# Transposing the inverse factors on VectorE in 32x32 blocks instead of on TensorE

## The chip, the cores and the metric

The kernel runs on one core of a Trainium2 chip. The metric is device time in microseconds, the median of three runs. TensorE, VectorE, ScalarE and GpSimd run side by side; SyncE issues loads. In the trace PE is TensorE, DVE VectorE, ACT ScalarE and POOL GpSimd.

## The reference

The program is three blocks one after the other on 256 tokens of width 2048: a gated delta network, a gated feed-forward, and a hybrid layer. The change lies in the first, in the part that solves a unit lower triangular system for each of 32 heads and each chunk of tokens:

```python
idx = jnp.arange(C)
lower = idx[:, None] >= idx[None, :]
strict = idx[:, None] > idx[None, :]
...
L = jnp.where(strict, jnp.einsum('bhnid,bhnjd->bhnij', kb, k) * decay, 0.0)
rhs = jnp.concatenate([v * beta[..., None], kb * jnp.exp(gc)[..., None]], -1)
sol = lax.linalg.triangular_solve(L + jnp.eye(C, dtype=L.dtype), rhs, left_side=True,
                                  lower=True, unit_diagonal=True)
```

The kernel works on chunks of 128 tokens and inverts I + L by levels: it knows the inverse on the diagonal blocks of size 1, and a level s = 2, 4, ..., 64 makes from the inverse on blocks of size s the one on blocks of size 2s, as T - T (L T) restricted to the new corner.

## The kernel before

**Stages.** The delta network's projection is walked in groups of 24 weight chunks. A chunk is 24 matmuls of 128x128 by 128x256 (or 12 of 128x512, lines 936, 923 and 955). Weights come as fp32 and are split: ScalarE copies a chunk to its high part (`gh`, line 1599), GpSimd subtracts it for the low part (`low`, line 662, `wl = wr - wh`), and TensorE multiplies with both. Buffers of high and low parts are three deep (`RING`), so the copy for chunk c + 3 waits for TensorE to have finished chunk c, and chunk c of the next group waits for GpSimd.

**Delta iterations.** Beside the chunks of group j + 1 runs the delta step of group j, eight iterations in all (`delta` on each engine). TensorE takes one chunk, one delta step, one chunk, and so on (`beside`, line 1182), with three chunks without a step behind them. In the seven first iterations all of this sits under the next group's projection; in the last one under the output projection. In-between work stands on the other engines in a fixed order written by hand: VectorE does its part of a delta step, then at steps 5 to 7 and 13 to 15 four operations of the convolution (`conv`, line 2158), then at steps 2 to 15 one mod half, two scalar_tensor_tensor of 128x512 that sum a modulation row out of SBUF (`mods`, line 2087). ScalarE does its chunk copy and then its delta part at the times in `STEP_AT`. GpSimd does the low part and at every second time issues a load of modulation weights (line 651).

**The levels.** For 4 heads and 2 token chunks there are 8 matrices, index n. `Tc` and `Uc` hold the two diagonal 64-blocks of the inverse and of its transpose, `lTb` the transposed L, `Xc` the intermediate. Blocks b = 0, 1 lie in partitions 0 to 63 and 64 to 127. Per level s, TensorE does an X step (line 1078: 16 products of 64x64), VectorE masks it from PSUM to `Xc` (line 2241, name `x`), TensorE multiplies `Uc` with it (line 1096, name `tx`), VectorE subtracts it from `Tc` (line 2246, name `t`), and TensorE transposes the new `Tc` (line 849, name `u`) in the step that also holds the next level's X; ScalarE brings the transpose from PSUM into `Uc` (line 1713). At s = 32 the transposition is done in blocks of 64 (line 1108). Before level 2 the first factors are made: `lm` masks L into `Uc` (line 2223), TensorE flips it (`flip_blocks`, line 1059, name `t2`), VectorE subtracts it from the identity into `Tc` (line 2233) and subtracts `Uc` from the identity in place (line 2236, `uc`).

**Quarters.** A 64x64 product uses the quarter of TensorE's array given by the partitions it reads and those it writes. `crossed` puts the results of level 2 in the half they came from, so only two quarters work; from level 4 on, block b of matrix n is put in half n % 2, so all four work in turn.

## Time and profile before

| | us |
|---|---|
| median of three runs | 2718.45 (2718.34 to 2719.01) |
| the profiled execution, first to last instruction | 2717.0 |
| TensorE busy (matmuls) | 2678.4 |
| VectorE busy | 1909.8 |
| ScalarE busy | 1212.6 |
| GpSimd busy | 854.2 |
| an iteration of the delta stage, second to seventh | 96.6 |

The eight delta iterations lie between about 160 and 930 us. TensorE's granted clock is full through the whole execution. A timeline row is a merged run of instructions of one kind: its length goes from the first start to the last end, and matmuls overlap, so the spacing of starts says more than the lengths. A matmul on fp32 data counts as two instructions.

### The profile page before, as it was taken

Reading aid. Unit: us, or ns where it says so; the run is one execution under the profiler, and the core shown is the slowest. Engines: PE = TensorE matmul, PEld = TensorE weight load, DVE = VectorE, ACT = ScalarE, POOL = GpSimd, SP = SyncE. Lnnn points to the kernel's source line nnn. Section 1 sums busy time; section 2 is a strip of 40 time slices with the busy share of each in tenths; the row PEclk is TensorE's granted clock in tenths of the full one; section 3 lists DMA queues with packets and bytes.
Section 4 is the critical chain, followed back from the end, with each engine's and each line's share of the span. In section 5 each row is a group of like instructions: output and inputs, shape, how many; then the busy total and the mean of one; then the engine's idle time right before and its main releaser. Section 6 shows DMA issues by size and latency. Waiting matters only on the chain.

```text
span 2717.0 us, 45293 instructions
## 1 busy us (share of the span) xinstructions
PE 2678.4 (99%) x17387; PEld 2250.4 (83%) x17387; DVE 1909.8 (70%) x2190; ACT 1212.6 (45%) x1572; POOL 854.2 (31%) x646
## 2 busy tenths in 40 slices
PE   6999999999999999999999999999999999999998
PEld 4798998899898888888888888889777778888887
DVE  1476777787787687666666666588999997655554
ACT  2355455545546445333333333354433334444344
POOL 1076676676667412600000000004565550000000
PEclk9999999999999999999999999999999999999999
DMA  9966666676665676666666666655555556666664
GB/s 364 354 219 207 227 225 204 223 239 200 224 229 188 219 223 228 189 187 186 187 190 188 190 186 186 185 162 172 171 179 170 161 173 187 192 186 186 192 202 155
DMA packets 283976, 552.53 MB, mean 203 GB/s; under 512 B 16882, under 2 KB 54323, under 8 KB 282675
## 3 DMA queue, kind: packets, MB, share of 16 engines
q1 hardware_dynamic: 263488, 473.49, 56.5%
q0 software_dynamic: 19472, 76.06, 7.4%
q8 instruction: 116, 1.90, 0.3%
q10 hardware_dynamic: 866, 0.80, 0.1%
q14 instruction: 34, 0.27, 0.0%
HBM read 548.19 MB, written 2.10 MB: 203 GB/s over the span
## 4 chain that ended last, share of the span: by engine, by line
PE 96%; DMA 2%; DVE 1%; SPq 1%; ACT 0%; issue 0%; DVEq 0%
PE pg L1220 40%; PE pd L1220 18%; PE pg L936 13%; PE pg L923 6%; PE pg L1207 4%; PE pg L955 3%; PE pd L849 2%; DMA wr<-in_gdn_w_in 1%; PE pd L1096 1%; PE pd L1078 1%; PE pd L1415 1%; PE pd L1428 1%; DMA arena<-in_mod_w 1%; PE pg L849 1%; PE pd L1027 1%; PE pd L1010 1%
## 5 line engine op out<-in xcount | busy, mean ns | idle before, releaser
L2341 DVE TENSOR_TENSOR wl<-wr,wh 128x1024 fp32r<-128x1024 f32 x615 | 773.7, 1268 | 453.7 <-ACT wh L1818 451.2
L1818 ACT ACTIVATE wh<-wr 128x1024 fp32r<-128x1024 f32 x616 | 652.8, 1061 | 936.2 <-PE pg L1220 590.3
L662 POOL TENSOR_TENSOR wl<-wr,wh 128x1024 fp32r<-128x1024 f32 x195 | 478.9, 2458 | 366.3 <-ACT wh L1599 231.3
L1220 PE MATMUL pg<-wh,hh 128*128 128x512 f32 x1344 | 529.8, 394 | 0.3 <-DVE hl L2414 0.3
L1220 PE MATMUL pg<-wl,hh 128*128 128x512 f32 x1344 | 527.3, 392 | 0.0
L1220 PE MATMUL pg<-wh,hl 128*128 128x512 f32 x1344 | 525.7, 391 | 0.0
L1599 ACT ACTIVATE wh<-wr 128x1024 fp32r<-128x1024 f32 x216 | 227.7, 1057 | 356.4 <-PE pg L936 196.4
L1220 PEld LDWEIGHTS pg<-wh,hh 128*128 128x128 f32 x1344 | 252.6, 188 | 59.1 <-DVE wl L2341 2.4
L936 PE MATMUL pg<-hh,wh 128*128 128x256 f32 x1024 | 300.7, 294 | 0.8 <-ACT arena L1659 0.8
L1220 PEld LDWEIGHTS pg<-wh,hl 128*128 128x128 f32 x1344 | 252.5, 188 | 56.3
L1220 PEld LDWEIGHTS pg<-wl,hh 128*128 128x128 f32 x1344 | 252.3, 188 | 53.9
L936 PE MATMUL pg<-hl,wh 128*128 128x256 f32 x1024 | 290.2, 283 | 0.0
L936 PE MATMUL pg<-hh,wl 128*128 128x256 f32 x1024 | 290.0, 283 | 0.0
L2087 DVE SCALAR_TENSOR_TENSOR arena<-arena,condt 128x512 f32<-128x512 f32 x225 | 250.2, 1112 | 20.3 <-DMA arena<-in_mod_w 14.8
L819 POOL COPY arena<-arena 128x2048 f32<-128x2048 f32 x1 | 2.7, 2662 | 671.9 <-PE pd L849 671.9
L936 PEld LDWEIGHTS pg<-hh,wh 128*128 128x128 f32 x1024 | 196.6, 192 | 16.3 <-issue 7.2
L936 PEld LDWEIGHTS pg<-hl,wh 128*128 128x128 f32 x1024 | 197.0, 192 | 0.5 <-issue 0.2
L936 PEld LDWEIGHTS pg<-hh,wl 128*128 128x128 f32 x1024 | 196.7, 192 | 0.0
L1220 PE MATMUL pd<-wl,hgh 128*128 128x512 f32 x320 | 125.5, 392 | 0.0
L1220 PE MATMUL pd<-wh,hgh 128*128 128x512 f32 x320 | 125.5, 392 | 0.0
L1220 PE MATMUL pd<-wh,hgl 128*128 128x512 f32 x320 | 125.1, 391 | 0.0
L773 POOL DMA_DIRECT2D xT<-in_final_g x1 | 0.6, 572 | 340.3 <-PE pd L1220 340.3
(446 smaller groups left out, 4727.3 us busy)
## 6 DMA issues: line engine op xcount, KB each, us to landing
wr<-in_w_in SPq DMA_DIRECT2D x224, 512.0 KB, 3.8
wr<-in_ffn_w_gu SPq DMA_DIRECT2D x176, 512.0 KB, 3.8
wr<-in_gdn_w_in SPq DMA_DIRECT2D x128, 512.0 KB, 4.1
arena<-in_mod_w POOLq DMA_DIRECT2D x60, 1024.0 KB, 6.7
wr<-in_ffn_w_down SPq DMA_DIRECT2D x88, 512.0 KB, 4.6
arena<-in_mod_w SPq DMA_DIRECT2D x32, 1024.0 KB, 13.7
wr<-in_gdn_w_in SPq DMA_DIRECT2D x128, 256.0 KB, 3.1
wr<-in_gdn_w_out SPq DMA_DIRECT2D x56, 512.0 KB, 4.5
```

What stands on the lines that cost most here:

```text
L662: nc.gpsimd.tensor_tensor(wl[c % RING][:], wraw[c % 4], wh[c % RING][:].bitcast(F32), ALU.subtract)\
L849: return nc.tensor.transpose(dst, src, ident[0:n, 0:n])
L923: m = nc.tensor.matmul(halves(bank)[:, t, :], h_s[x][:, 2 * kp + k, t * P:(t + 1) * P], w[c % RING][:, k, :], skip_group_check=True, start ...
L936: m = nc.tensor.matmul(bank[:, n * T:(n + 1) * T], w[c % RING][:, k, n * P:(n + 1) * P], h_s[x][:, 2 * kp + k, :], skip_group_check=True, ...
L955: m = nc.tensor.matmul(halves(pg[g])[:, h, :], o_s[x][:, 2 * kp + k, h * P:(h + 1) * P], w[c % RING][:, k, :], skip_group_check=True, star ...
L1010: m = nc.tensor.matmul(pd[0][:, n * 512:(n + 1) * 512], ones[:], sqb[:, n * 512:(n + 1) * 512], start=True, stop=True)
L1207: m = nc.tensor.matmul(bank[:, n * T:(n + 1) * T], w[s][:, k, n * P:(n + 1) * P], act[x][:, k0 + k, :], skip_group_check=True, start=(firs ...
L1220: m = nc.tensor.matmul(halves(bank)[:, h, :], act[x][:, k0 + k, h * P:(h + 1) * P], w[s][:, k, :], skip_group_check=True, start=(first and ...
L1599: a(wh[c % RING][:], wraw[c % 4], ACT.Copy).then_inc(s_hi, 1)
L1818: a(wh[c % 4][:], wraw[c % 4], ACT.Copy).then_inc(s_hc, 1)
L2087: m = stt(out=dst, in0=mw[t % 2][:, k, :], scalar=condt[:, kk:kk + 1], in1=dst, op0=ALU.mult, op1=ALU.add)
L2341: v.tensor_tensor(wl[c % 4][:], wraw[c % 4], wh[c % 4][:].bitcast(F32), ALU.subtract).then_inc(s_lc, 1)
```

## The change

Up to blocks of 32, the transpose of `Tc` is made by VectorE with one instruction that transposes every 32x32 block where it stands: the factors have nothing outside their diagonal 32-blocks then. The transposed factors stand in `Us`, the right half of `Ub`. TensorE reads a factor from `Us` where block b and half n % 2 agree, and else from `Uc`, where ScalarE puts it by two copies that cross the partition halves (`cross`). Products of level 2 use the same placement as the later ones. The flip of the first factor and the transpositions after t2, t4, t8 and t16 go from TensorE's program; with two results fewer per level, `pd[1]` always holds X and `pd[0]` the product. The masked L goes to `Us`, the identity is subtracted there (`us1`), and VectorE transposes it to `Tc`. The name and wait lists (`PEO`, `VO`, `AO`) change with it. Level 32 and what follows stay.

```diff
-PEO = order("ssq", "rows", "gram", "ktok", "t2", "x2", "tx2", "u2", "x4", "tx4", "u4", "x8",
-            "tx8", "u8", "x16", "tx16", "u16", "x32", "tx32", "u32", "x64", "ux64", "v0", "md0", "s", "o0", "r",
-            "qs", "v1", "o1", "md1")
-VO = order("qn", "qkn", "dt", "lt", "lm", "at", "tc", "uc", *[f"{a}{s}" for s in LEVELS for a in ("x", "t")],
+PEO = order("ssq", "rows", "gram", "ktok", "vt1", *[f"{a}{s}" for s in LEVELS for a in ("x", "tx")],
+            "u32", "x64", "ux64", "v0", "md0", "s", "o0", "r", "qs", "v1", "o1", "md1")
+VO = order("qn", "qkn", "dt", "lt", "lm", "at", "us1", "tc",
+           *[f"{a}{s}" for s in LEVELS for a in (("x", "t", "us") if s < 32 else ("x", "t"))],
            "x64", "u64", "md0", "o0", "rhs1", "o1", "oz", "md1", "on", "og")
-AO = order("rnq", "rn", "exp", "kg", "vtok", "z", *[f"u{s}" for s in LEVELS], "v0", "s", "qs", "v1", "qkv", "rstd")
+AO = order("rnq", "rn", "exp", "kg", "vtok", "u1", "z", *[f"u{s}" for s in LEVELS], "v0", "s", "qs", "v1", "qkv", "rstd")
 GO = order("rowm")
...
@@ -222,6 +222,7 @@
         Tb = take(8, P)
         Xc = Xb.rearrange("p a b -> p (a b)")[:, 0:512].rearrange("p (n t) -> p n t", t=64)
         Ub = take(8, P)
+        Us = Ub[:, :, 64:P]
         Tc, Uc = (Tb.rearrange("p a b -> p (a b)")[:, 512 * i:512 * (i + 1)].rearrange("p (n t) -> p n t", t=64)
                   for i in range(2))
...
@@ -1036,7 +1037,6 @@
                     m = tr(pd[0][:, 512 + h * P:512 + (h + 1) * P], vT[:, h, 0:P])
                 m.then_inc(s_pe, 1)
                 yield
-                V("lm")
                 Ac("kg")
 
...
-                def crossed(s, b, n):
-
-                    return (b, slot(n)) if s == 2 else (n % 2, 4 * b + n // 2)
+                def crossed(b, n):
+
+                    return n % 2, 4 * b + n // 2
+
+                def u_block(b, n):
+
+                    r = slice(64 * (n % 2), 64 * (n % 2) + 64)
+                    return Us[r, n, :] if n % 2 == b else Uc[r, n // 2, :]
 
                 def each_block():
                     for m in range(4):
                         yield from ((0, 2 * m), (1, 2 * m + 1), (0, 2 * m + 1), (1, 2 * m))
 
-                def flip_blocks(bank, src, at):
-                    for n in range(8):
-                        for b in range(2):
-                            r = slice(64 * b, 64 * b + 64)
-                            m = nc.tensor.matmul(block(bank, b, slot(n)), src[r, at(n), :], ident[r, r],
-                                                 start=True, stop=True)
-                    return m
-                flip_blocks(pd[0], Uc, slot)
...
-                par = 1
...
                     else:
                         for b, n in each_block():
                             r = slice(64 * b, 64 * b + 64)
-                            m = nc.tensor.matmul(block(pd[par], *crossed(s, b, n)), lTb[r, n, r], Tc[r, n, :],
+                            m = nc.tensor.matmul(block(pd[1], *crossed(b, n)), lTb[r, n, r], Tc[r, n, :],
                                                  start=True, stop=True)
...
                 for s in LEVELS:
                     V(f"x{s}")
-                    if s > 2:
-                        Ac(f"u{s // 2}")
-                    else:
-                        V("uc")
+                    Ac(f"u{s // 2}")
+                    if s == 2:
                         Ac("vtok")
-                    par ^= 1
                     for b, n in each_block():
-                        half, i = crossed(s, b, n)
+                        half, i = crossed(b, n)
                         r = slice(64 * half, 64 * half + 64)
-                        m = nc.tensor.matmul(block(pd[par], b, slot(n)), Uc[r, i, :], Xc[r, i, :], start=True, stop=True)
+                        m = nc.tensor.matmul(block(pd[0], b, slot(n)), u_block(b, n), Xc[r, i, :], start=True, stop=True)
                     m.then_inc(s_pe, 1)
                     yield
                     V(f"t{s}")
-                    par ^= 1
-                    if s < 32:
-                        for m in range(4):
-                            t = tr(pd[par][:, m * P:(m + 1) * P], Tc[:, 2 * m:2 * m + 2, :])
-                    else:
+                    if s == 32:
                         for n in range(8):
...
                         for n in range(0, 8, 2):
-                            t = nc.tensor.matmul(pd[par][0:64, 512 + 32 * n:576 + 32 * n], Tc[64:P, n, :],
+                            t = nc.tensor.matmul(pd[1][0:64, 512 + 32 * n:576 + 32 * n], Tc[64:P, n, :],
                                                  ident[64:P, 64:P], start=True, stop=True)
-                    t.then_inc(s_pe, 1)
-                    par ^= 1
+                        t.then_inc(s_pe, 1)
...
@@ -1700,25 +1686,29 @@
                     a(kg0[:, h, :], pd[0][:, (h // 2) * P:(h // 2 + 1) * P], ACT.Copy, scale=tkc[:, 6, h:h + 1])
                 a(vtok[:, 0:VH, :].rearrange("p a b -> p (a b)"), pd[0][:, 512:1024], ACT.Copy).then_inc(s_a, 1)
                 yield
-                V("tc")
+                PEw("vt1")
                 a(vtok[:, VH:8, :].rearrange("p (a b) t -> p a (b t)", a=2),
                   pd[0][:].rearrange("p (a c) -> p a c", a=2)[:, :, 256:512], ACT.Copy).then_inc(s_a, 1)
+
+                def cross(s):
+
+                    V(f"us{s}")
+                    a(Uc[0:64, 0:4, :], heads(Us)[64:P, :, 0, :], ACT.Copy)
+                    a(Uc[64:P, 0:4, :], heads(Us)[0:64, :, 1, :], ACT.Copy).then_inc(s_a, 1)
+                cross(1)
                 yield
                 silu_z(it)
                 yield
-                par = 1
                 for s in LEVELS:
-                    PEw(f"u{s}")
                     if s < 32:
-                        a(four(Uc).rearrange("p b m t -> p m b t"),
-                          pd[par][:, 0:512].rearrange("p (m b t) -> p m b t", b=2, t=64), ACT.Copy).then_inc(s_a, 1)
+                        cross(s)
                     else:
+                        PEw("u32")
                         for b in range(2):
                             r = slice(64 * b, 64 * b + 64)
-                            a(Ub[r, :, r], pd[par][r, 0:512].rearrange("p (n t) -> p n t", t=64), ACT.Copy)
-                        a(Uc[0:64, 0:4, :], pd[par][0:64, 512:768].rearrange("p (n t) -> p n t", t=64), ACT.Copy)\
+                            a(Ub[r, :, r], pd[1][r, 0:512].rearrange("p (n t) -> p n t", t=64), ACT.Copy)
+                        a(Uc[0:64, 0:4, :], pd[1][0:64, 512:768].rearrange("p (n t) -> p n t", t=64), ACT.Copy)\
                             .then_inc(s_a, 1)
-                    par ^= 1
                     yield
                 PEw("v0")
                 for h in range(VH):
...
                     r = slice(64 * b, 64 * b + 64)
-                    m = v.tensor_tensor(by_n(four(Uc[r])), heads(lTb[r, :, r]),
-                                        m1t[r, 0:64].unsqueeze(1).unsqueeze(1).broadcast_to([64, 4, 2, 64]), ALU.mult)
+                    m = v.tensor_tensor(Us[r], lTb[r, :, r], m1t[r, 0:64].unsqueeze(1).broadcast_to([64, 8, 64]),
+                                        ALU.mult)
...
                 yield
-                PEw("t2")
-                done(v.tensor_tensor(heads(Tc), identc.unsqueeze(1).unsqueeze(1).broadcast_to([P, 4, 2, 64]),
-                                     by_n(compact(pd[0])), ALU.subtract))
                 dve.wait_ge(s_v, bv + VO["lm"])
-                done(v.tensor_tensor(Uc, identc.unsqueeze(1).broadcast_to([P, 8, 64]), Uc, ALU.subtract))
-                yield
-                par = 1
+                done(v.tensor_tensor(Us, identc.unsqueeze(1).broadcast_to([P, 8, 64]), Us, ALU.subtract))
+                dve.wait_ge(s_v, bv + VO["us1"])
+                done(v.transpose(Tc, Us))
+                yield
                 for s in LEVELS:
                     PEw(f"x{s}")
-                    done(v.tensor_tensor(four(Xc), compact(pd[par]),
+                    done(v.tensor_tensor(four(Xc), compact(pd[1]),
                                          msk[s][:, 0:64].unsqueeze(1).unsqueeze(1).broadcast_to([P, 2, 4, 64]), ALU.mult))
-                    par ^= 1
                     yield
                     PEw(f"tx{s}")
-                    done(v.tensor_tensor(heads(Tc), heads(Tc), by_n(compact(pd[par])), ALU.subtract))
-                    par ^= 1
-                    par ^= 1
+                    done(v.tensor_tensor(heads(Tc), heads(Tc), by_n(compact(pd[0])), ALU.subtract))
+                    if s < 32:
+                        dve.wait_ge(s_v, bv + VO[f"t{s}"])
+                        done(v.transpose(Us, Tc))
...
```

## Rows read from the trace of the kernel before

**Rows 1.** The page: busy time, share of the span, instructions.
```profile
PE 2678.4 (99%) x17387; PEld 2250.4 (83%) x17387; DVE 1909.8 (70%) x2190; ACT 1212.6 (45%) x1572; POOL 854.2 (31%) x646
```
**Rows 2.** Waits of TensorE and VectorE: total us, times, longest.
```profile
PE pd L1096 <- DVE arena L2241: 0.8, 1, 0.8
...
DVE arena L2241 <- PE pd L1078: 9.2, 15, 3.0
...
DVE arena L2246 <- PE pd L1096: 1.8, 7, 0.4
```
**Rows 3.** Timeline of TensorE, fifth iteration, fourth level: start us, us, instructions.
```profile
575.73 0.28 PE L936 MATMUL pg<-hh,wl 128*128 128x256 f32 x1
575.85 0.60 PE L849 MATMUL pd<-ident,arena 128*128 128x128 f32 x4
576.37 0.69 PE L1078 MATMUL pd<-arena 64*64 64x64 f32 x32
577.00 0.39 PE L936 MATMUL pg<-hh,wh 128*128 128x256 f32 x1
...
579.86 0.28 PE L936 MATMUL pg<-hh,wl 128*128 128x256 f32 x1
580.07 0.69 PE L1096 MATMUL pd<-arena 64*64 64x64 f32 x32
580.69 0.39 PE L936 MATMUL pg<-hh,wh 128*128 128x256 f32 x1
```
**Rows 4.** Timeline of TensorE: flips, fifth iteration; first level, eighth iteration.
```profile
563.11 1.15 PE L1059 MATMUL pd<-ident,arena 64*64 64x64 f32 x32
...
564.60 0.36 PE L936 MATMUL pg<-hh,wh 128*128 128x256 f32 x1
...
856.46 1.15 PE L1078 MATMUL pd<-arena 64*64 64x64 f32 x32
```
**Rows 5.** Busy us over the ten level steps: PE, PEld, DVE, ACT, POOL.
```profile
567.64:607.15 39.51, 39.51 (x567) 36.73 (x566) 34.98 (x44) 17.79 (x24) 27.18 (x16) 1.00 0.79 270
```
**Rows 6.** Timeline of VectorE, fifth iteration.
```profile
562.27 1.42 DVE L2227 TENSOR_TENSOR arena<-pd,arena 128x256 f32<-128x256 f32 x4
...
565.49 2.19 DVE L2236 TENSOR_TENSOR arena<-masks,arena 128x512 f32<-128x512 f32 x1
567.60 1.53 DVE L2087 SCALAR_TENSOR_TENSOR arena<-arena,condt 128x512 f32<-128x512 f32 x2
...
569.86 2.87 DVE L2087 SCALAR_TENSOR_TENSOR arena<-arena,condt 128x512 f32<-128x512 f32 x2
...
577.14 0.69 DVE L2241 TENSOR_TENSOR arena<-pd,masks 128x512 f32<-128x512 f32 x1 [0.36 <-PE pd L1078]
577.75 1.65 DVE L2158 SCALAR_TENSOR_TENSOR arena<-pg,arena 128x255 f32<-128x255 f32 x4
```
**Rows 7.** Timeline of GpSimd and ScalarE, fifth iteration.
```profile
562.40 4.73 POOL L662 TENSOR_TENSOR wl<-wr,wh 128x1024 fp32r<-128x1024 f32 x2 [1.41 <-DVE arena L2223]
...
568.89 2.50 POOL L662 TENSOR_TENSOR wl<-wr,wh 128x1024 fp32r<-128x1024 f32 x1 [1.03 <-ACT wh L1599]
...
571.89 1.06 ACT L1599 ACTIVATE wh<-wr 128x1024 fp32r<-128x1024 f32 x1 [0.72 <-PE pg L936]
```
**Rows 8.** Timeline of ScalarE, seventh iteration: a quarter copy.
```profile
802.98 0.38 ACT L1719 ACTIVATE arena<-pd 64x256 f32<-64x256 f32 x1
```
**Rows 9.** Groups by form: count, busy us, mean ns, idle before.
```profile
L2407 DVE TENSOR_SCALAR arena<-arena 128x512 f32<-128x512 f32 x12 | 6.0, 542 | 0.0
```
**Rows 10.** Timeline of VectorE and GpSimd, first iteration.
```profile
181.35 2.96 DVE L2087 SCALAR_TENSOR_TENSOR arena<-arena,condt 128x512 f32<-128x512 f32 x1
...
181.37 2.40 POOL L662 TENSOR_TENSOR wl<-wr,wh 128x1024 fp32r<-128x1024 f32 x1 [0.52 <-ACT wh L1599]
```

More of the change, by code:

```diff
@@ L1072, in x_step @@
                         for n in range(8):
-                            m = nc.tensor.matmul(block(pd[par], n % 2, n // 2), lTb[0:64, n, 64:P], Tc[0:64, n, :],
+                            m = nc.tensor.matmul(block(pd[0], n % 2, n // 2), lTb[0:64, n, 64:P], Tc[0:64, n, :],
                                                  start=True, stop=True)
@@ L1107, in delta @@
                                 r = slice(64 * b, 64 * b + 64)
-                                t = nc.tensor.matmul(pd[par][r, 64 * n:64 * n + 64], Tc[r, n, :], ident[r, r],
+                                t = nc.tensor.matmul(pd[1][r, 64 * n:64 * n + 64], Tc[r, n, :], ident[r, r],
                                                      start=True, stop=True)
                         for n in range(0, 8, 2):
-                            t = nc.tensor.matmul(pd[par][0:64, 512 + 32 * n:576 + 32 * n], Tc[64:P, n, :],
+                            t = nc.tensor.matmul(pd[1][0:64, 512 + 32 * n:576 + 32 * n], Tc[64:P, n, :],
                                                  ident[64:P, 64:P], start=True, stop=True)
-                    t.then_inc(s_pe, 1)
-                    par ^= 1
+                        t.then_inc(s_pe, 1)
                     x_step(2 * s)
@@ L1122, in delta @@
                     u = Ub[r, n, 64:P] if n % 2 else Uc[r, n // 2, :]
-                    m = nc.tensor.matmul(block(pd[par], 0, slot(n)), Xc[r, n // 2, :], u, start=True, stop=True)
+                    m = nc.tensor.matmul(block(pd[1], 0, slot(n)), Xc[r, n // 2, :], u, start=True, stop=True)
                 m.then_inc(s_pe, 1)
-                assert par == 1
                 yield
@@ L2231, in delta @@
                 yield
-                PEw("t2")
-                done(v.tensor_tensor(heads(Tc), identc.unsqueeze(1).unsqueeze(1).broadcast_to([P, 4, 2, 64]),
-                                     by_n(compact(pd[0])), ALU.subtract))
                 dve.wait_ge(s_v, bv + VO["lm"])
-                done(v.tensor_tensor(Uc, identc.unsqueeze(1).broadcast_to([P, 8, 64]), Uc, ALU.subtract))
+                done(v.tensor_tensor(Us, identc.unsqueeze(1).broadcast_to([P, 8, 64]), Us, ALU.subtract))
+                dve.wait_ge(s_v, bv + VO["us1"])
+                done(v.transpose(Tc, Us))
                 yield
-                par = 1
                 for s in LEVELS:
                     PEw(f"x{s}")
-                    done(v.tensor_tensor(four(Xc), compact(pd[par]),
+                    done(v.tensor_tensor(four(Xc), compact(pd[1]),
                                          msk[s][:, 0:64].unsqueeze(1).unsqueeze(1).broadcast_to([P, 2, 4, 64]), ALU.mult))
-                    par ^= 1
                     yield
                     PEw(f"tx{s}")
-                    done(v.tensor_tensor(heads(Tc), heads(Tc), by_n(compact(pd[par])), ALU.subtract))
-                    par ^= 1
-                    par ^= 1
+                    done(v.tensor_tensor(heads(Tc), heads(Tc), by_n(compact(pd[0])), ALU.subtract))
+                    if s < 32:
+                        dve.wait_ge(s_v, bv + VO[f"t{s}"])
+                        done(v.transpose(Us, Tc))
                     yield
                 PEw("x64")
-                done(v.tensor_copy(Xc[:, 0:4, :].rearrange("p a b -> p (a b)"), pd[par][:, 0:256]))
+                done(v.tensor_copy(Xc[:, 0:4, :].rearrange("p a b -> p (a b)"), pd[0][:, 0:256]))
                 yield
```

## The prediction

> **What bounds the kernel now.** I read the busy table first. TensorE is busy for 2678.4 us of a span of 2717.0, VectorE for 1909.8, GpSimd for 854.2 [rows 1]. So every TensorE instruction taken out is worth its time, as long as nobody makes TensorE wait. Next came TensorE's waits: in the level steps of eight iterations its matmuls wait for VectorE once, 0.8 us [rows 2]. Last came the timelines of the fifth iteration (550 to 646 us), which stands for iterations 2 to 6. TensorE alternates a weight chunk (24 matmuls) with one delta step; while the chunk runs, VectorE must turn the step's PSUM result into the operand of the next step. In the ten level steps, 567.64 to 607.15, VectorE is busy for 34.98 of 39.51 us and GpSimd for 27.18 [rows 5]. So TensorE sets the pace there, with VectorE close behind, and the gain is decided by whether VectorE keeps up.
>
> **What TensorE loses.** (a) A t-step: chunk matmul at 575.73, transposes at 575.85, X step at 576.37, next chunk at 577.00, a gap of 1.27; the step without transposes goes 579.86 to 580.69, a gap of 0.83 [rows 3]. Four of them: 4 x 0.44 = 1.76 us per iteration. (b) The first level's two block steps go from two quarters (1.15 us [rows 4]) to four (0.69 [rows 3]): 2 x 0.46 = 0.92. (c) The flip of the first factor: 563.11 to 564.60, or 1.49 us, for the flips and four transposes of v [rows 4]; four transposes alone take 575.85 to 576.37, or 0.52 [rows 3], so 0.97 goes. Sum 1.76 + 0.92 + 0.97 = 3.65 us per iteration, 29.2 in eight. With TensorE never waiting the span would be 2687.8.
>
> **What the others get.** ScalarE: four evictions of PSUM become five pairs of quarter copies, 0.38 us each by the nearest one [rows 8]; ScalarE does them behind its chunk copy and is busy for only 17.79 of the 39.51 us [rows 5], so they cost nothing; were that cover gone, 0.76 us for each of five, 3.8 per iteration. VectorE: the subtraction from PSUM (0.69) becomes a transposition in front of the first product, and four more transpositions follow t2 to t16. No row shows one. Lower bound: the cheapest 128x512 operation of one SBUF input, 0.54 [rows 9]; upper: one that has to wait out GpSimd, 2.19 [rows 6]. I take 0.69, as the 128x512 product of X4, which has one operand in SBUF [rows 6], since the transposition reads one tensor. So 4 x 0.69 = 2.8 us are added to an engine that has 39.51 - 34.98 = 4.5 us left in a stretch which is to shrink by 1.76 + 0.92 = 2.7. Behind each transposition on VectorE's queue stand the mod halves (two scalar_tensor_tensor) and, after t4, a part of the convolution of 1.65 us [rows 6]; the next product stands behind those, and TensorE waits for that.
>
> **The port.** A mod half has both tensors in SBUF. Alone the pair takes 1.53 us; beside GpSimd's low part of a chunk (2.40) the same pair takes 2.87, and 569.86 + 2.87 ends 1.33 after that low part (568.89 + 2.50), which is 0.54 for the first and 0.79 for the second [rows 6, 7]. The row of 181.35 shows one alone: 2.96 us for an operation of 0.75, with GpSimd's low part issued 0.02 later and running its plain 2.40 [rows 10]. So the two exclude each other, and one at the head of its queue gets in between two of the other's. One step then needs 2.40 + 1.50 = 3.9 us of the two engines together. A step lasts 3.95 now (39.51 over ten) and would last 3.70 (576.37 to 580.07, a step with no transposes in it [rows 3]). The Trainium skill, SBUF — State Buffer, section Who interferes with whom, says that an operation of two SBUF inputs and a GpSimd one that reads SBUF hold the shared pair exclusively, and one of a single SBUF input does not contend; the first is what these rows show, the second is what 0.69 for the transposition assumes. A page's price, in the skill's VectorE: DVE Perf Modes, The three transpose paths, is 311 ns for 128x128 bf16; taken four times it is an estimated 1.24 us, which would add 0.55 to each of the transpositions and 2.2 us to an iteration.
>
> **The fifth iteration walked through.** The "at" products end at 562.27 + 1.42 = 563.7. TensorE's short v step lets the next chunk start at 563.5 and X2 at 566.5 (before: 567.64). The identity subtraction us1 (two SBUF inputs) gets the port between the two low parts that start at 562.40, ends at 565.3, and the transposition at 566.0: on time. But the second low part now ends at 567.6, so the first mod pair ends at 568.9, X2's product at 569.5. The next low part runs 568.75 to 571.15, and the first operation of the next pair ends at 571.7. TensorE's chunk ended at 569.96; ScalarE's copy follows 0.35 later and takes 1.06, so GpSimd issues at 571.4, before VectorE's second operation at 571.7 (before the change: ScalarE's copy ran 571.89 to 572.95 [rows 7], and the pair was over at 572.73). The low part wins until 573.95, the pair ends at 574.5, t2 at 575.1; TensorE wanted it at 573.9 and waits 1.2 us. From there each wait delays the chunk behind it only by as much, so the low part again lands inside the pair. I get a spacing of 4.4 us for steps whose VectorE part is the product and 4.9 for those with a transposition, against 3.70. The step after the ten starts at 611.4; it did at 607.15, and would without waits at 603.5. Two variants: if GpSimd keeps the port for its two low parts in a row, X2 is 2 us late at once, the jam returns with x8 (t4 has transposition and convolution ahead of its mods) and the end is 610.4; if the jam resolves at x16, where the two issue within 0.1 us of each other, 609.4. So iterations 1 to 7 lose between 2.2 and 4.3 us each against now: I take 3.1. The later steps have room and neither add nor give back. The last iteration has no convolution and mods in every second step only, so it keeps its saving of 3.65.
>
> **The forecast.** 7 x 3.1 - 3.65 = +18.0 on 2717.0 gives 2735.0; the median of the runs lies 1.45 above the span, so 2736.5. Range of this case: 7 x 1 - 3.65 = +3 to 7 x (4.3 + 2.2) - 3.65 = +42, or 2722 to 2760. Chance 0.49.
>
> **Rivals.** (1) VectorE keeps up throughout: 2718.45 - 29.2 = 2689.3. For it: of the 80 products in the level steps only 22 waited for TensorE (15 and 7 [rows 2]), yet TensorE waited once, since there is room: X4's product ends at 577.83 and the next step starts at 580.07, 2.2 us later [rows 3, 6]; against it: that room is spent by 0.44 less pitch and 0.69 more work at each t-step. With a wait of up to 1 us per iteration it reaches 2697. Chance 0.23. (2) The port fills but never jams: the ten steps take 3.9 instead of 3.70, 2.0 us of wait per iteration, so 7 x (3.65 - 2.0) + 3.65 = 15.2 saved: 2703.3; between 2697 and 2713. For it: where a mod pair falls wholly between two low parts it takes 1.53 now; against it: that needs the two queues to interleave cleanly at x4 to t8, with convolutions of 1.65 us in between. Chance 0.20. This turns into the forecast at the point where the waits pass 3.65 us per iteration. (3) Waits and saving cancel, 2713 to 2724: chance 0.08. That the change doesn't take out what it says is excluded by its code.
>
> **How the numbers follow.** The likeliest case gives 2736.5. For 8 in 10 the range has to reach to the first rival, 2689, and up to 2756, short of the full slower transposition. What a measurement of this kernel can tell from no change is about 0.2%, or 5.4 us. Faster by more: 0.23 + 0.20 = 0.43; within: 0.08; slower: 0.49. The two signs share the chance almost evenly, so the forecast's own range, 2722 to 2760, should be read beside it.
>
> **What the profile after would show.** TensorE's waits hold lines for VectorE's two level products, about 7 us per iteration, and its busy time falls all the same. The transposition rows have 0.69 us; with over 1 us the loss is larger; with GpSimd's low part beside them and 2 us or more, they hold the port too. The gap of a t-step without wait is 0.83. Mod operations of 2 to 3 us in the level steps become more frequent, since the pair is split by a low part. If TensorE's waits are under 1 us per iteration, the walk is wrong at 571.4 against 571.7, or at t4. What would also make it wrong: a transposition far from 0.69, or a ScalarE copy that comes late enough to let VectorE's pair through.

## The result and the profile after

The changed kernel takes 2773.92 us (median of four runs, 2771.93 to 2775.43) against 2718.41 for the kernel before: ratio 1.0203, 95% interval 1.0189 to 1.0216. It is slower by 55 us. The forecast was slower by 18 (2736.5), and the range ended at 2756. The profiled execution spans 2770.7 us, 53.7 more than before. One of the six executions of run 13 below took 3417.42 us at a granted clock of 0.72; the median there is 2705.18 with it and 2705.10 without.

The page's busy line (answers to [rows 1]), and TensorE's waits for VectorE in the delta stage (total us, times, longest; they answer to [rows 2]). L1089 is the second product of a level (tx), L1074 the first (x), L1122 the product behind the last level, L1097 the flips:
```profile
PE 2660.1 (96%) x17003; PEld 2229.1 (80%) x17003; DVE 2006.6 (72%) x2222; ACT 1229.5 (44%) x1620; POOL 872.1 (31%) x646
...
PE pd L1089 <- DVE arena L2229: 45.0, 31, 2.7
PE pd L1074 <- DVE arena L2233: 13.4, 19, 2.4
PE pd L1122 <- DVE arena L2242: 9.1, 5, 1.8
PE pd L1097 <- DVE arena L2233: 4.3, 7, 0.6
```
TensorE issues 384 matmuls fewer and is busy for 18.3 us less, but the time in which it is not busy grows from 38.6 to 110.6 us. 72.0 - 18.3 = 53.7. The four waits, 71.8 us in all where there was one of 0.8, account for 71.0 of the 72.0 us.

The groups by operation (total us, mean ns, idle before):
```profile
L2077 DVE SCALAR_TENSOR_TENSOR arena<-arena,condt 128x512 f32<-128x512 f32 x225 | 322.5, 1433 | 5.5
...
L2236 DVE STREAM_TRANSPOSE arena<-arena 128x512 f32<-128x512 f32 x32 | 22.8, 711 | 1.1
...
L1696 ACT ACTIVATE arena<-arena 64x256 f32<-64x256 f32 x40 | 16.7, 417 | 10.6 <-DVE arena L2236 5.4 <-DVE arena L2223 4.0
```
The new operations cost what was expected: 0.71 us for a transposition, 0.42 for a quarter copy, and TensorE never waits for the copies. What grew is an operation that the change does not touch: the modulation sums take 1433 ns each, against 1112 before, 72 us more on VectorE.

Where a jam begins, in the timelines of VectorE, GpSimd and TensorE, fifth iteration (start us, us). They answer to [rows 6, 7]:
```profile
594.23 1.75 DVE L2223 TENSOR_TENSOR arena<-masks,arena 128x512 f32<-128x512 f32 x1
596.01 0.71 DVE L2225 STREAM_TRANSPOSE arena<-arena 128x512 f32<-128x512 f32 x1
596.65 2.13 DVE L2077 SCALAR_TENSOR_TENSOR arena<-arena,condt 128x512 f32<-128x512 f32 x1
598.81 3.14 DVE L2077 SCALAR_TENSOR_TENSOR arena<-arena,condt 128x512 f32<-128x512 f32 x1
602.08 0.69 DVE L2229 TENSOR_TENSOR arena<-pd,masks 128x512 f32<-128x512 f32 x1
...
593.02 5.21 POOL L663 TENSOR_TENSOR wl<-wr,wh 128x1024 fp32r<-128x1024 f32 x2 [1.41 <-DVE arena L2213]
598.17 0.80 POOL L652 DMA_DIRECT2D arena<-in_mod_w  x1
598.99 2.40 POOL L663 TENSOR_TENSOR wl<-wr,wh 128x1024 fp32r<-128x1024 f32 x1
...
602.82 0.69 PE L1089 MATMUL pd<-arena 64*64 64x64 f32 x32 [2.02 <-DVE arena L2229]
```
The identity subtraction (L2223) gets in between two low parts, the transposition (L2225) follows at once, and TensorE does X2 at 597.04: all on time. The first modulation sum (596.65) then waits out the second low part. The second is issued at 598.81, 0.18 us before GpSimd's next low part, and yet takes 3.14 us, while the low part runs its plain 2.40. X2's product on VectorE starts at 602.08, and TensorE stands for 2.02 us. t2, x4 and t4 are not waited for; from x8 on (620.56) six more waits of 0.5 to 1.4 us follow in the level steps and one of 1.84 behind them (653.47). This iteration's waits add up to 9.4 us.

**Who gets the port.** Counted over all the traces kept here, for sums that begin while no low part runs, up to 0.74 us before the next one begins:
- The low part begins 0.05 us or more after GpSimd's last instruction: 806 of 806 sums begun more than 0.05 us before it went through in 0.71 to 0.75 us, and 15 of 16 begun at most 0.05 us before it took 2.94 us or more, [rows 10] among them.
- The low part follows a DMA issue of GpSimd directly, by 0.02 us: of 59 sums begun up to 0.70 us before it, 54 took 2.9 us or more. The sum at 598.81 is one, and so are those behind X2 in the other iterations from the second to the seventh (begun 0.16 to 0.18 us before the low part).

So a sum begun a little earlier holds up a low part that comes out of a wait, and loses to one that stands directly behind a DMA issue. A sum that loses ends 0.54 to 0.56 us after the low part. No run changed that one thing alone (a pause between issue and low part, say), so this is a count, and its reason stays open.

TensorE's clock, in the windows of 2 us in the second iteration (length, busy of PE, PEld, DVE, ACT, POOL, granted clock, DMA share, GB/s):
```profile
286.00:288.00 2.00, 1.63 (x14) 1.42 (x12) 2.00 (x1) 1.73 (x3) 2.00 (x1) 1.00 0.82 201
288.00:290.00 2.00, 0.34 (x21) 0.35 (x25) 1.88 (x3) 2.00 (x5) 1.43 (x2) 1.00 1.05 424
290.00:292.00 2.00, 2.00 (x32) 1.93 (x25) 1.96 (x2) 0.18 (x1) 1.16 (x1) 0.60 1.01 377
292.00:294.00 2.00, 2.00 (x12) 2.00 (x11) 1.84 (x4) 0.00 (x0) 0.77 (x1) 0.55 0.90 250
```
TensorE idles from 287.63 to 289.65 and, from 290.39 on, works for 3.4 us at 1.2 instead of 2.4 GHz. Between 150 and 960 us this happens six times, each time 0.7 to 1.6 us behind an idle stretch of 1.7 us or more (thirteen such stretches in all; seven leave the clock alone). Length times missing clock is 10.2 us; before has no such stretch there. (The section on the profile before calls its clock full throughout. It is not: from 38.7 to 48.9 us, and for short stretches at 1793 and 2711 us, it is at the lower level, and the changed kernel has the like. None of these lies in the delta stage.) The 10.2 us are most of why TensorE's busy time fell by 18.3 us and not by 29.2. They are not all extra: in iterations 2, 3, 5 and 7 such a stretch stands behind X2's product, the jam pauses until x8, and the waits in the level steps are 7.0 to 7.6 us; in 4 and 6 the clock stays full there, the jam goes on at x4, and they are 9.6.

### The profile page after: what moved, and what is told of

It reads as the page before. It is cut to its first block, busy times and chain, and to the rows that moved or that the text cites. A ratio compares the mean times of both kernels' runs of the same rounds, so it can differ in the third digit from the quotient of the medians.

```text
span 2770.7 us, 44627 instructions
## 1 busy us (share of the span) xinstructions
PE 2660.1 (96%) x17003; PEld 2229.1 (80%) x17003; DVE 2006.6 (72%) x2222; ACT 1229.5 (44%) x1620; POOL 872.1 (31%) x646
## 4 chain that ended last, share of the span: by engine, by line
PE 78%; DVE 18%; DMA 2%; issue 1%; SPq 1%; ACT 0%; DVEq 0%
PE pg L1206 39%; PE pd L1206 18%; DVE arena L2077 10%; PE pg L924 4%; PE pg L1193 4%; PE pg L937 3%; DVE arena L2148 2%; PE pg L956 1%; DMA wr<-in_gdn_w_in 1%; PE pd L850 1%; DVE arena L2229 1%; DVE arena L2075 1%; DVE arena L2213 1%; DVE arena L2233 1%; DVE arena L2207 1%
## 5 line engine op out<-in xcount | busy, mean ns | idle before, releaser
L663 POOL TENSOR_TENSOR wl<-wr,wh 128x1024 fp32r<-128x1024 f32 x195 | 495.3, 2543 | 351.8 <-ACT wh L1585 215.4
L2077 DVE SCALAR_TENSOR_TENSOR arena<-arena,condt 128x512 f32<-128x512 f32 x225 | 322.5, 1433 | 5.5
```

Source lines behind the costliest of these rows:

```text
L663: nc.gpsimd.tensor_tensor(wl[c % RING][:], wraw[c % 4], wh[c % RING][:].bitcast(F32), ALU.subtract)\
L2077: m = stt(out=dst, in0=mw[t % 2][:, k, :], scalar=condt[:, kk:kk + 1], in1=dst, op0=ALU.mult, op1=ALU.add)
```

## Experiments

The theories. **Port**: the modulation sums (two operands in SBUF) and GpSimd's low parts exclude each other; the change leaves too little room for both, a sum loses to a low part, and every step behind it is late. **Length**: VectorE simply has 0.7 us per transposition too much to do, whatever it contends with. **Seed**: the jam is started by a sum standing right behind a transposition, and goes away if that sum stands elsewhere. Times are single ones for the runs 1 to 11 (before beside them: 2722.36 for 1 to 4, 2719.59 for 5 to 8, 2718.29 for 9 to 11), and medians of 5 to 12 executions for 12 to 15 (before: 2718.83, then 2719.22).

**1. The four level transpositions left out.**
```diff
-                        done(v.transpose(Us, Tc))
+                    (left out; the subtraction counts for both)
```


> The changed kernel without VectorE's four transpositions after t2, t4, t8 and t16 (left out, so the factors it multiplies with are stale); the waits for them are met by the subtraction before. First theory (the port: mod pairs and GpSimd's low parts exclude each other, and the shorter step makes them collide): the four times 0.71 us are only part of it, TensorE still waits for VectorE several us per iteration, 2725 to 2760. Rival (VectorE simply has too much to do, and the transpositions are what is too much): without them TensorE's waits are gone, 2690 to 2700.

2737.53 us. 34.8 us of span come back for 22.8 us of transpositions, so these cost more than their length. But 40.5 us of waits stay (25.4 at L1089, 9.6 at L1074, 5.5 behind the levels), and X2's product still starts 4.35 us after X2 has ended in iterations 2 to 6, and 4.06 in the seventh, as in the changed kernel. The level transpositions did not start that jam.

**2 and 3. The modulation sums replaced by transpositions, in the changed kernel and in the one before.**
```diff
-                        m = stt(out=dst, in0=mw[t % 2][:, k, :], scalar=condt[:, kk:kk + 1], in1=dst,
-                                op0=ALU.mult, op1=ALU.add)
+                    m = v.transpose(dst, mw[t % 2][:, k, :])
```


> The changed kernel with each modulation operation of iterations 1 to 7, and of the last, of 128x512 (two SBUF inputs, 0.75 us alone) replaced by a transposition of the same size (one SBUF input, 0.71 us), so the modulation sums are left out; VectorE's work stays within 1.5 us per iteration. Port theory: the operations of 2 to 3 us vanish, TensorE's waits fall from 72 us to under 10, 2685 to 2700. Rival (too much work on VectorE): hardly better than the change, 2755 to 2772.

> The kernel before with the same replacement of the modulation operations (sums left out). Both theories: TensorE hardly waits in the kernel before, so the time stays at 2716 to 2719; VectorE's busy time falls by about 80 us, since 225 operations of 1.11 us become 0.71. It is the base for the run of the changed kernel with the same replacement: the difference of the two is what the change brings TensorE, forecast at 29 us.

2688.23 and 2717.70 us. The replacement has one SBUF operand and takes nearly as long as a sum alone, as its group in run 2 shows, above the two busy lines (run 2, then run 3):
```profile
L2074 DVE STREAM_TRANSPOSE arena<-arena 128x512 f32<-128x512 f32 x240 | 169.8, 707 | 41.5 <-DMA arena<-in_mod_w 36.0
...
PE 2647.0 (99%) x17003; PEld 2222.0 (83%) x17003; DVE 1823.7 (68%) x2222; ACT 1229.4 (46%) x1620; POOL 854.2 (32%) x646
```
```profile
PE 2677.8 (99%) x17387; PEld 2250.9 (83%) x17387; DVE 1797.9 (66%) x2190; ACT 1212.0 (45%) x1572; POOL 851.7 (31%) x646
```
In the kernel before this is worth nothing against its own profile (2716.1 against 2717.0 of span); in the changed one it takes away 84 us and all but three of the waits for VectorE in the level steps (0.82, 0.28 and 0.15 us are left). VectorE has as many instructions (2222) as the changed kernel. A replaced operation is only 0.04 us shorter than a sum that runs alone, so this is the port, not the length. The difference of the two runs, 29.5 us, is what the change saves when nothing jams; the sum of the prediction was 29.2.

**4. The kernel before with four unused transpositions behind t2 to t16.**
```diff
+                    if s < 32:
+                        dve.wait_ge(s_v, bv + VO[f"t{s}"])
+                        v.transpose(Ub[:, :, 64:P], Tc)
```


> The kernel before with four transpositions on VectorE added after t2, t4, t8 and t16, whose results nobody reads; TensorE's work stays. Work theory: 8 x 4 x 0.71 = 23 us more on VectorE jams this kernel too, 2735 or more. Port theory with the shorter step as a needed part: at the longer steps of this kernel (room of 2.0 to 2.4 us at each product) most of it is covered, 2718 to 2728.

2729.24 us, 1.2 above the second range. Iterations 2 to 7 keep their period of 96.6 us; the first iteration alone jams (107.5) and carries the loss. So, from the second iteration on, VectorE has room for the four transpositions at the old pace of TensorE. Their cost appears together with the faster pace.

**5. The pace given back: TensorE does four unused transposes at each t-step of the changed kernel.**
```diff
+                    if s < 32:
+                        for m in range(4):
+                            tr(pd[0][:, m * P:(m + 1) * P], Tc[:, 2 * m:2 * m + 2, :])
```


> The changed kernel with four transpositions on TensorE put back after t2, t4, t8 and t16 (into a bank nobody reads), so that its steps there are as long as before, with VectorE's work unchanged. Shorter-step theory: 14 us come back as TensorE work, but the low parts come later and the jam at x4 to x32 loosens, so the time falls against the change, 2735 to 2760. Rival (VectorE's work alone sets the pace in the jam): TensorE's extra work hides in its waits and the time stays at 2770 to 2776.

2757.67 us, 16 less than the changed kernel, though TensorE has more to do. Waits of 22.2 us at L1089 and 12.1 before the added transposes stay. The wait of 2.0 us at X2's product (1.7 in the seventh) stands in iterations 2 to 7; the edit changes nothing in front of it. Behind it the slower pace lets the jam clear in four of them (3, 4, 6 and 7, with no other wait for VectorE in the level steps) and not in 2 and 5, nor in the first: 97 to 98 us an iteration against 108.

**6. The sums of iterations 1 to 7 one step later, GpSimd's loads for them one low part later.**
```diff
-                for half in (0, 1) if t == 0 else (t,) if 2 <= t < 16 else ():
+                for half in (0, 1) if t == 0 else (t - 1,) if 3 <= t < 17 else ():
-                    elif t >= 6 and t % 2 == 0 and t <= 16:
+                    elif t >= 7 and t % 2 and t <= 17:
```


> The changed kernel with the fourteen modulation halves of iterations 1 to 7 each one step later (steps 3 to 16 instead of 2 to 15, their loads too), so that none stands between the first transposition and X2's product. Seed theory (the jam starts at the pair behind the first transposition): X2's product is on time, the first wait of 2 us and the stretch at the low clock behind it vanish, the jam then starts at x8 behind t4; 2735 to 2760. Rival (a saturated stretch jams wherever the mods stand): within 5 us of the change.

2734.97 us, 39 less than the changed kernel, with the same instructions. X2's product now starts 0.07 us after X2 has ended in iterations 1 to 7. The jam starts at x8 (in two iterations at t4), behind the t4 step, where a transposition, a convolution part and a pair of sums stand in a row: its first sum holds up the low part begun 0.16 us later, and its second waits that low part out (VectorE, then GpSimd, fifth iteration):
```profile
593.75 0.75 DVE L2077 SCALAR_TENSOR_TENSOR arena<-arena,condt 128x512 f32<-128x512 f32 x1
594.53 2.77 DVE L2077 SCALAR_TENSOR_TENSOR arena<-arena,condt 128x512 f32<-128x512 f32 x1
...
593.91 2.84 POOL L663 TENSOR_TENSOR wl<-wr,wh 128x1024 fp32r<-128x1024 f32 x1 [1.02 <-ACT wh L1585]
```

**7. A schedule by hand: no sums at steps 7 and 12, two halves at step 15.**
```diff
+MOD_AT = {0: (0, 1), 3: (2,), 4: (3,), 5: (4,), 6: (5,), 8: (6,), 9: (7,), 10: (8,), 11: (9,), 13: (10,), 14: (11,),
+          15: (12, 13), 16: (14, 15)}
+MOD_LOADS = {6: 2, 9: 3, 11: 4, 14: 5, 16: 6, 19: 7}
```


> The changed kernel with the modulation halves retimed: ten instead of twelve in the steps that feed TensorE's levels (none at the first product, none at steps 7 and 12), four behind the levels at steps 15 and 16; their loads follow. Port theory: a step with a pair needs 3.9 us of the port against 3.70, one without gives 1.3 back, so the jam can clear and most of the saving appears, 2690 to 2715. Rival (VectorE's total work): the same work in the same stretch less two pairs, 2750 to 2765.

2741.2 us: a miss, and worse than run 6. X2's jam is gone, but in iterations 2 to 6 t2, x4, t4 and x8 jam, and two halves in one step bring 9.5 us of waits for the step behind (L1151).

**8 and 9. t2 and t4 transposed by TensorE as before, the rest as changed; then the same with run 6's edit.**
```diff
+                    if s < 8:
+                        for m in range(4):
+                            t = tr(pd[0][:, m * P:(m + 1) * P], Tc[:, 2 * m:2 * m + 2, :])
+                        t.then_inc(s_pe, 1)
```


> The change in part: the transposes after t2 and t4 stay on TensorE and ScalarE as before, those of the first factor and after t8 and t16 go to VectorE, first level on four quarters. It saves TensorE 0.97 + 0.92 + 2 x 0.44 = 2.8 us per iteration, 22 us. Port theory: the jam's seed at X2 is still there, but no transposition stands in front of the convolution at t4; waits of 3 to 5 us per iteration, 2715 to 2740. Rival (the transpositions at t2 and t4 were the whole trouble): 2696 to 2700.

> The change in part (transposes after t2 and t4 stay on TensorE, those of the first factor and after t8 and t16 go to VectorE, first level on four quarters), and the modulation halves of iterations 1 to 7 one step later. Both seeds seen so far are gone: the pair behind the first transposition, and the pair behind transposition and convolution at t4. Port theory: TensorE's waits in iterations 1 to 7 all but vanish; the saving of 22 us shows but for the last iteration, 2698 to 2712. Rival (each such fix only moves the jam elsewhere): 2720 or more.

2734.41 and 2709.85 us, both in the range of the port theory. In run 8 X2's wait of 2.0 us stands in iterations 2 to 6. In run 9 it is gone; 13.1 us of waits are left, none of them in iterations 1, 4, 5 and 6.

**10 and 13. Only the first factor transposed by VectorE, all of t2 to t16 by TensorE, with run 6's edit** (the same diff with `s < 32`; run 13 is the code of run 10 again).

> Only the first factor is transposed on VectorE, every later transpose stays on TensorE and ScalarE; first level on four quarters; modulation halves one step later. TensorE is spared 0.97 + 0.92 = 1.9 us per iteration, 15 us, and VectorE has no work that it did not have before. Port theory: no jam in iterations 1 to 7, 2703 to 2708. Rival (the shorter steps alone jam it): 2715 or more.

> The same code as e10, timed in rounds beside e12 on one chip: only the first factor is transposed on VectorE, the first level takes four quarters, the modulation halves stand one step later. If the port is what matters, the version that asks least of VectorE is at least as fast as the one that makes the whole change: 2705 to 2708 us, 0.38 to 0.49% under before. If the four transpositions that it leaves on TensorE cost more than the port gives back, e12 beats it by over 1.5 us.

2706.32 and 2705.18 us; the latter is a median of six, against 2718.83, ratio 0.9949, interval 0.9936 to 0.9962. It is the fastest version found. 13.6 us of gain stand against (2 x 0.46 + 0.97) x 8 = 15.1 by the terms (b) and (c) of the prediction's sum. Of the waits for VectorE in the delta stage one of 2.2 and one of 0.6 us are left in run 13. No run makes run 6's edit alone in the kernel before, so what it adds to this gain is not shown.

**11. The whole change, sums one step later, none at step 6 (t4), two halves at step 16.**
```diff
+MOD_AT = {0: (0, 1), 3: (2,), 4: (3,), 5: (4,), 7: (5,), 8: (6,), 9: (7,), 10: (8,), 11: (9,), 12: (10,), 13: (11,),
+          14: (12,), 15: (13,), 16: (14, 15)}
+MOD_LOADS = {7: 2, 9: 3, 12: 4, 14: 5, 16: 6, 18: 7}
```


> The whole change, modulation halves one step later and none at step 6 (behind t4, where transposition and convolution stand), one more at step 16. Port theory: the jam that the run with halves one step later had from x8 on is gone too, 2695 to 2715. Rival (work on VectorE: the stretch from x2 to t8 has more than TensorE's time allows): the jam starts elsewhere, 2725 to 2740.

2707.86 us, once. The level steps of iterations 2 to 7 run free, with periods of 92.7 to 95.2 us; 16.5 us of waits are left, 12.3 of them in the first and the last iteration. This looked like the cure. It is not a robust one, as the next runs show.

**12. Run 11 with VectorE's own operations of the last iteration moved away from t2 and t4.**
```diff
-LATE_LOWS = (0, 1, 2, 4, 6)
-LATE_HALVES = (0, 3, 5, 7, 9, 11, 12, 13)
+LATE_LOWS = (0, 1, 3, 5, 7)
+LATE_HALVES = (0, 3, 7, 9, 11, 12, 13, 14)
```


> Same kernel as the run that skips the pair behind the t4 step (e11), and in the last iteration, which has operations of its own, the two low-part operations of VectorE that stood right behind the t2 and t4 steps' transpositions stand behind X2, X4 and X8 instead, with the mod halves of these places moved behind. If the jam that is left in the last iteration (X4 was served 4.9 us late in e11) came from a long two-operand operation standing right behind a transposition, TensorE's wait at the products of the last iteration falls from about 3.6 us to under 1 and the kernel takes 2703 to 2705 us. If it came from GpSimd's two low parts in a row there, which no order on VectorE changes, the wait only moves to another step and the time stays at 2706 to 2709. Against before (2718.4) both are faster, by 0.35 to 0.57%.

2716.68 us (twelve runs, 2712.46 to 2728.41), ratio 0.9997, interval 0.9986 to 1.0008: no gain at all, and outside both forecasts. In the last iteration x2 to x32 take 34.3 us against 34.2, so the waits only moved: the level products are served, and TensorE waits for the low parts of the output projection instead (2.1 us for GpSimd's, 1.2 and 0.7 for VectorE's). The spread is the news. In this profile the first iteration jams as in run 11, and the fourth and the sixth as well, whose code is that of the others. The sixth, at the x4 to t4 steps, on VectorE and then GpSimd:
```profile
668.84 0.75 DVE L2080 SCALAR_TENSOR_TENSOR arena<-arena,condt 128x512 f32<-128x512 f32 x1 [0.47 <-DMA arena<-in_mod_w]
...
669.63 2.94 DVE L2080 SCALAR_TENSOR_TENSOR arena<-arena,condt 128x512 f32<-128x512 f32 x1
...
669.63 2.40 POOL L666 TENSOR_TENSOR wl<-wr,wh 128x1024 fp32r<-128x1024 f32 x1 [0.57 <-ACT wh L1588]
```
The load of the modulation weights landed late enough that the pair began 0.47 us after VectorE was free. Its second sum met a low part in the same hundredth and lost 2.2 us; in the fifth iteration the pair began 0.12 us after the convolution and got through. TensorE then waits at t4, t8, x16, t16 and x32, and the iteration takes 101.5 us where the fifth took 92.7.

**14 and 15. The load that was late issued one low part earlier, in run 12's and in run 11's kernel.**
```diff
-MOD_LOADS = {7: 2, 9: 3, 12: 4, 14: 5, 16: 6, 18: 7}
+MOD_LOADS = {6: 2, 9: 3, 12: 4, 14: 5, 16: 6, 18: 7}
```


> e12 with one change: GpSimd issues the modulation load of each iteration whose first half is used at the X4 step one low part earlier, about 3.7 us. In e12 its product started 0.47 us after the ScalarE-free point because the load landed then (iteration 6, 668.84 us), the pair's second operation tied with a low part at 669.63, lost 2.2 us, and the jam stayed for the rest of that iteration (about 9 us); in iteration 5 it landed in time and nothing jammed. If a load landing late is what decides, iterations 2 to 7 all run free at the t4 step, the times lie closer together than e12's 2712 to 2728 us, and the median falls to 2706 to 2710 us. A late load at the X32 step (e12, 496.21 us) is not mended by this and may still cost one iteration some 5 us. If the jams come by chance whatever the loads do, the median stays at 2714 to 2719 us.

> e11 with the same load moved, so with the last iteration as the change has it. If moving the last iteration's own operations was worth nothing (in e12 the wait only went to another step), this is within 1.5 us of e14. If they were worth their 3 us, e14 is 2 to 4 us faster. If the load decides, it is also at or under e11's one time, 2707.86 us.

2767.04 and 2765.22 us. Not 10 us better but 50 worse, from one DMA issue per iteration that moved by 3.7 us. The pair behind X2 in run 12 (fifth iteration), VectorE and GpSimd:
```profile
565.96 2.83 DVE L2080 SCALAR_TENSOR_TENSOR arena<-arena,condt 128x512 f32<-128x512 f32 x1
568.83 0.75 DVE L2080 SCALAR_TENSOR_TENSOR arena<-arena,condt 128x512 f32<-128x512 f32 x1
...
562.94 5.31 POOL L666 TENSOR_TENSOR wl<-wr,wh 128x1024 fp32r<-128x1024 f32 x2
568.19 0.80 POOL L655 DMA_DIRECT2D arena<-in_mod_w  x1
569.54 2.40 POOL L666 TENSOR_TENSOR wl<-wr,wh 128x1024 fp32r<-128x1024 f32 x1 [0.56 <-ACT wh L1588]
```
and in run 14:
```profile
595.05 3.55 DVE L2080 SCALAR_TENSOR_TENSOR arena<-arena,condt 128x512 f32<-128x512 f32 x1
598.64 2.93 DVE L2080 SCALAR_TENSOR_TENSOR arena<-arena,condt 128x512 f32<-128x512 f32 x1
...
594.82 0.80 POOL L655 DMA_DIRECT2D arena<-in_mod_w  x1
595.64 2.41 POOL L666 TENSOR_TENSOR wl<-wr,wh 128x1024 fp32r<-128x1024 f32 x1
598.62 2.40 POOL L666 TENSOR_TENSOR wl<-wr,wh 128x1024 fp32r<-128x1024 f32 x1 [0.57 <-ACT wh L1588]
```
In run 12 GpSimd's DMA issue of 0.80 and its wait for ScalarE stand between two low parts, 1.3 us in which the second sum passes in 0.75. In run 14 the issue stands one place earlier. The first sum, begun inside it and 0.59 before the low part that follows it directly, loses to that low part; the gap behind is only 0.57, and the second sum is issued 0.02 after the next low part and loses too. Iterations 2 to 6 jam from t2 on, all five. So the seed theory holds in part only: run 6 had moved the sums and the loads together, and run 14 shows that with the sums where run 6 had them the place of one load alone decides for t2. Run 15 against run 14 shows again that the last iteration's reordering brings nothing.

## Why the prediction was right and wrong

**The direction and the mechanism** held: TensorE saves, the port fills, and the waits outweigh the saving. Runs 2 and 3 show the port as the cause, because taking the second SBUF operand away removes all of the loss. The forecast gave a slower kernel 0.49, and its walk had the first jam in another place, so that the sign came out right is in part luck.

**The savings** (29.2 us): 29.5 between runs 2 and 3. **ScalarE's copies** at nothing: no wait for them. **The transposition** at 0.69: 0.71, and it does not wait out the low part. The trace agrees with both things that the prediction takes from **the Trainium skill**, SBUF — State Buffer, Who interferes with whom: sums of two SBUF operands, which exclude a low part, went from 1112 to 1433 ns, and transpositions, which read one, stayed at 0.71. The prediction's estimate of 1.24 us, from the bf16 figure in the Trainium skill's VectorE: DVE Perf Modes, The three transpose paths, was far too high for this fp32 block; no run supports the 2.2 us per iteration that it put into the upper end of the range.

**The spacing in a jam** (4.4 and 4.9, or 9.3 us for two steps): from x8 to x32 in the fifth iteration TensorE's tx products start 9.3 us apart for every two steps (620.56, 629.84, 639.11).

**What failed: the size of the waits, in both terms of 7 x 3.1 - 3.65 = +18.0.** From the first X2 to the last it is 52.0 us longer than before (7.4 per iteration, not 3.1), and outside that stretch 1.8 us longer, where the last iteration was to give 3.65 back; 52.0 + 1.8 is the 53.7 seen, but for rounding.
- The term 3.1 was picked from a range whose upper end, 4.3, was the walk's own result (7.9 us of waits less 3.65 saved). In the level steps of iterations 1 to 7 TensorE waited 7.0 to 9.7 us, 8.4 on average, against 6.75 in the forecast: 11.5 us of the 36 missing. There the walk was nearly right, though not by its own path, as the next point shows.
- The walk lets the first pair of sums pass at 568.9 with the next low part at 568.75, and puts the first jam one pair later. In the trace GpSimd's low part came 0.76 us after the previous one had ended, not 1.15 as in the walk, because ScalarE's copy was already there and only the DMA issue of 0.80 stood between. The sum that had been issued 0.18 earlier lost. [rows 10] held a like case already (issued 0.02 earlier, at a low part that came out of a wait, and lost), and the walk gave the port to whoever was issued first all the same. X2's product ended 5.7 us after X2 started, not 3.0; TensorE waited 2.0 there. One of the walk's two variants (X2 2 us late at once, the jam back with x8) describes iterations 2, 3, 5 and 7.
- "The later steps have room" is false: TensorE waits 1.84 us in front of L1122, 9.1 us in all. "It keeps its saving", of the last iteration, as well: TensorE waits 4.1 us there, 2.7 of them behind an operation of its own that begins beside two low parts in a row and takes 5.53 us (914.31; it takes 1.2 us where it meets none). Together the waits are 9.0 us per iteration over eight, against some 6.75 over seven in the forecast: 71.8 against 47.
- The clock was left out: 10.2 us of slow TensorE behind the longer waits, some of which spare waits in their turn, as told above.

The sum with measured terms is 71.8 of waits - 0.8 of before - 29.5 + 10.2 = 51.7, of the 53.7 seen. The forecast was 47.2 - 29.2 = 18.

**The range** ended at 2756 (2760 for the forecast's own case) because the walk put the loss of an iteration at 2.2 to 4.3 us against before; it was 6.4 to 9.3 in iterations 2 to 6. With the whole change an iteration takes 92.7 to 95.2 us where the level steps do not jam, and 96.6 to 106 where they do, by where the jam starts (runs 6, 7, 11, 12, 14, 15 and the changed kernel). With the same operations the time was 2773.92 us, and 2707.86 once, and which iterations jam hangs on 0.02 to 0.5 us (runs 12 and 14). A range for such a kernel has to hold both ends.

**What stays open.** What starts the first iteration's jam at t4, which is there in runs 11, 12, 14 and 15 alike, was not tried. Why seven of thirteen idle stretches of 1.7 us or more left the clock alone isn't explained. What the slow clock is worth on balance is not shown either: no run holds it fixed. And no run tries the pause between a DMA issue and the low part behind it, where the sums behind X2 were lost in the changed kernel.

## What to carry to other kernels

Before you move work to an engine, add up what it and its port partner need per step of the pace that you are about to set; the work that you move may be harmless, while the faster pace makes two old neighbours collide. Where the sum is near the step, read who is issued when in one step to the hundredth, DMA issues included, and give a range that holds both the kernel without a jam and the one that jams in every iteration; give the saving only where slack is left (here, the part of the change without the level transpositions, 0.5% faster). A single good time of a kernel in that condition proves little: 2707.86 once, 2712 to 2728 in twelve runs of nearly the same code.

## What the runs showed of the hardware

- A two-operand operation of VectorE begun 0.18 us before GpSimd's low part took 3.14 us and the low part its plain 2.40 (598.81), where the low part followed a DMA issue of GpSimd by 0.02 us; 54 of 59 such sums lost, one begun 0.59 us before the low part among them (595.05 in run 14). Where the low part began 0.05 us or more after GpSimd's last instruction, all 806 sums begun more than 0.05 us before it went through.
- A transposition of 128x512 fp32 by VectorE takes 0.71 us, with GpSimd's low part running or not (240 of them at 707 ns on average in run 2, and 24 beside a low part and 16 without one in the changed kernel, all at 0.71 or 0.72).
- A sum that begins during GpSimd's DMA issue of 0.80 us takes its plain 0.75 if no low part stands directly behind the issue (568.83 in run 12). One issue per iteration, moved by one place, changed the time by 50 us (run 14 against run 12).
- Behind six of thirteen idle stretches of 1.7 to 2.7 us TensorE's granted clock fell to the 1.2 GHz level for 3.4 us; in the kernel before, which has no idle stretch over 1.5 us between 150 and 960 us, it did not fall there.
